# A decoder layer in FP32 on one core: the first two output-projection units begun together, the last two and the second norm in token halves

## What is computed

```python
merged = sigmoid(g_attn) * y_attn + sigmoid(g_pool) * y_pool     # (512, 1024)
x = x + gate1 * (merged @ w_out)                                  # w_out (1024, 1024)
h2 = rms_norm(x, norm2_g) * (1 + scale2) + shift2                 # mean of squares over the 1024 channels
up = h2 @ w_up                                                    # w_up (1024, 2 x 2816)
x = x + gate2 * ((silu(conv(up)_a) * conv(up)_b) @ w_down)
```

## Time and profile before

| | |
|---|---|
| median of 3 runs | 799.43 us (798.09 to 799.55) |
| span of the profiled execution, first to last instruction | 797.5 us |
| mean granted TensorE clock over the span | 0.989 |
| TensorE matmul busy | 97% |
| DVE, ACT, POOL busy | 47%, 38%, 44% |
| share of TensorE in the chain that ended last | 89% |

### The profile page before, as it was taken

The page is one execution under the profiler, slowest core; times in us unless marked ns, Lnnn a source line. Parts: engine busy times, 40 slices in busy tenths (PEclk is TensorE's granted clock), DMA queues, the critical chain, the costliest instruction groups (busy, mean ns, idle before and its releaser), DMA issues.

```text
span 797.5 us, 9523 instructions
## 1 busy us (share of the span) xinstructions
PE 772.9 (97%) x3618; PEld 622.3 (78%) x3618; DVE 371.7 (47%) x678; ACT 307.0 (38%) x492; POOL 353.5 (44%) x187
## 2 busy tenths in 40 slices
PE   4999999999999999998999999999999999999998
PEld 3367688887887888886886888888888888888886
DVE  2562399953656572448747444455443443000000
ACT  4234423346654553333233634434344344112121
POOL 1135258346534572354661544444344444444350
PEclk9979999999999999998999999999999999999999
DMA  8933112231043133454747333323333222232301
GB/s 322 356 106 107 53 53 67 94 106 44 10 159 106 53 110 102 151 165 159 227 143 263 106 106 106 95 74 95 106 106 95 78 93 93 92 106 93 120 27 53
DMA packets 94461, 91.72 MB, mean 115 GB/s; under 512 B 2003, under 2 KB 85711, under 8 KB 94415
## 3 DMA queue, kind: packets, MB, share of 16 engines
q1 hardware_dynamic: 92239, 82.71, 33.0%
q10 hardware_dynamic: 2176, 8.39, 3.1%
HBM read 89.00 MB, written 2.10 MB: 114 GB/s over the span
## 4 chain that ended last, share of the span: by engine, by line
PE 89%; DVE 7%; ACT 1%; issue 1%; DMA 1%; SPq 0%; ACTq 0%; DVEq 0%
PE bank L1368 49%; PE bank L1377 24%; PE bank L1589 3%; PE bank L1625 2%; DVE work L1153 2%; PE bank L1399 2%; DVE top L1150 2%; PE bank L1438 2%; PE bank L1600 2%; PE bank L1458 1%; PE bank L1404 1%; PE bank L1500 1%; DMA xn<-in_x_dram 1%; PE bank L1510 1%; DVE pmean L1187 1%
## 5 line engine op out<-in xcount | busy, mean ns | idle before, releaser
L583 POOL TENSOR_TENSOR wsplit<-stage,wsplit 128x1024 fp32r<-128x1024 f32 (+2 forms) x127 | 288.4, 2275 | 389.6 <-ACT wsplit L694 389.5
L1368 PE MATMUL bank<-hT,wsplit 128*128 128x512 f32 x1200 | 287.6, 391 | 0.0
L1368 PEld LDWEIGHTS bank<-hT,wsplit 128*128 128x128 f32 x1200 | 223.7, 188 | 46.6 <-issue 0.6
L694 ACT ACTIVATE wsplit<-stage 128x1024 fp32r<-128x1024 f32 (+2 forms) x127 | 125.6, 991 | 316.6 <-PE bank L1377 301.9
L1377 PE MATMUL bank<-hT,wsplit 128*128 128x512 f32 x600 | 150.8, 392 | 0.0
L1377 PEld LDWEIGHTS bank<-hT,wsplit 128*128 128x128 f32 x600 | 111.3, 188 | 24.2 <-issue 1.6
L1368 PE MATMUL bank<-guT,wsplit 128*128 128x512 f32 x352 | 84.0, 390 | 0.0
L1368 PEld LDWEIGHTS bank<-guT,wsplit 128*128 128x128 f32 x352 | 65.9, 188 | 13.5
L1330 DVE SCALAR_TENSOR_TENSOR yb<-bank,conv,yb 128x511 f32<-128x511 f32 (+1 forms) x44 | 33.0, 749 | 66.0 <-ACT yb L964 65.1
L1330 DVE SCALAR_TENSOR_TENSOR ya<-bank,conv,ya 128x511 f32<-128x511 f32 (+1 forms) x44 | 33.0, 750 | 60.1 <-ACT ya L964 59.4
L1355 DVE SCALAR_TENSOR_TENSOR xT<-bank,mod,xT 128x512 f32<-128x512 f32 x8 | 6.0, 751 | 111.5 <-PE bank L1377 111.5
(11 more groups left out here) (182 smaller groups left out, 837.4 us busy)
## 6 DMA issues: line engine op xcount, KB each, us to landing
stage<-in_w_up_dram SPq DMA_DIRECT2D x44, 512.0 KB, 5.2
stage<-in_w_in_dram SPq DMA_DIRECT2D x17, 1024.0 KB, 5.3
ada_mid<-in_w_ada_dram ACTq DMA_DIRECT2D x8, 1024.0 KB, 5.4
stage<-in_w_down_dram SPq DMA_DIRECT2D x8, 1024.0 KB, 5.1
ada<-in_w_ada_dram SPq DMA_DIRECT2D x7, 1024.0 KB, 12.3
stage<-in_w_ada_dram SPq DMA_DIRECT2D x4, 1024.0 KB, 5.6
stage<-in_w_out_dram SPq DMA_DIRECT2D x4, 1024.0 KB, 7.4
ada_last<-in_w_ada_dram SPq DMA_DIRECT2D x4, 1024.0 KB, 8.5
```

What stands on the lines that cost most here:

```text
L583: pool.tensor_tensor(unit_split(n, 1), unit_source(n), unit_split(n, 0).bitcast(F32), ALU.subtract).then_inc(low, 1)
L694: me.did(act.activation(unit_split(n, 0), unit_source(n), ACT.Copy), high)
L1368: pe.matmul(out_bank[:, :], hi[:, k, :], rhs[:, part, k0 + k, :], start=first and k == 0 and part == 0, stop=False)
```

## The change

**Head.** ("wo", 0) and ("wo", 1) are begun together, in three steps: blocks 0 to 5 of both, block 6 of both, block 7 of both. `mod_columns(3)` follows both. Orders on the other engines stay.

**Tail.** Units 6 and 7 are done for tokens 0 to 255 first (24 matmuls of 256 columns each), then `mod_columns(4)`, the squares of that half, then unit 6 for tokens 256 to 511 (into `PT[1]`), the roots of half 0, unit 7 for tokens 256 to 511 (into `PT[0]`). Residuals, squares, roots, norm and first up products are all done by halves; the up units 0 take half 0 with their low products two blocks behind, then half 1 with them one block behind. The squares of units 6 and 7 are summed by TensorE alone, so GpSimd adds five blocks instead of six. The units' `used` signal, which frees the ring, comes with their second half. `keep_clock` is gone.

**Both norms.** The square root takes scale 1/D and a bias tile `eps`, set by GpSimd at the start; the multiply-add ahead of it is gone.

```diff
@@ constants @@
+            pool.memset(eps[:, :], EPS).then_inc(consts, 1)
@@ gpsimd @@
-            for m in range(1, KD - 1):
+            for m in range(1, KD - 2):
                 low_parts(min(sch.unit["wo", m] + 3, sch.unit["wo", KD - 1] + 1))
@@ scalar @@
-            act.wait_ge(mean_ok, 1)
-            me.did(act.activation(tstat[:, 2, :], tstat[:, 1, :], ACT.Sqrt), root_ok)
+            def roots_of(n, tiles):
+                act.wait_ge(mean_ok, n)
+                me.did(act.activation(tstat[:, 2, tiles[0]:tiles[-1] + 1], tstat[:, 0, tiles[0]:tiles[-1] + 1],
+                                      ACT.Sqrt, bias=eps[:, 0:1], scale=1.0 / D), root_ok)
...
+            square_half(KD - 2, 0)
+            square_half(KD - 1, 0)
+            roots_of(2, HALF_TILES[0])
+            chunk(("wo", KD - 2))
+            square_half(KD - 2, 1)
+            for k in range(KD):
+                if k == 4:
+                    chunk(("wo", KD - 1))
+                    square_half(KD - 1, 1)
+                if k == KD - 1:
+                    roots_of(3, HALF_TILES[1])
+                h_high(KD + k, k, 3, HALVES[0])
+            for k in range(KD):
+                h_high(2 * KD + k, k, 3, HALVES[1])
@@ vector @@
+            for m in (KD - 2, KD - 1):
+                dve.wait_ge(wo_half, m - (KD - 2) + 1)
+                residual(m, 2, bank(("wo", m)), HALVES[0], x2_half)
             mod_vector(4)
+            half_roots(0)
+            await_chunk(dve, ("wo", KD - 2))
+            residual(KD - 2, 2, PT[1], HALVES[1], drained["dve"])
+            dve.wait_ge(root_b, 2)
             me.settle()
+            for k in range(KD):
+                norm_part(KD + k, k, 1, SC[0], HALVES[0])
+                if k:
+                    low_part(KD + k - 1, k - 1, 3, HALVES[0])
+                if k == 3:
+                    await_chunk(dve, ("wo", KD - 1))
+                    residual(KD - 1, 2, PT[0], HALVES[1], drained["dve"])
+            half_roots(1)
+            low_part(2 * KD - 1, KD - 1, 3, HALVES[0])
+            dve.wait_ge(root_b, 3)
...
@@ tensor @@
+            names = (("wo", 0), ("wo", 1))
+            for name in names:
+                await_bank(pe, name)
+            for ks in (range(KD - 2), range(KD - 2, KD - 1), range(KD - 1, KD)):
                 pe.wait_ge(m_lo, ks.stop)
-                high_products(sch.unit[first], bank(first), merged, ks=ks)
-                low_products(sch.unit[first], bank(first), merged, ks=ks)
-            for m in range(1, KD - 1):
+                for name in names:
+                    high_products(sch.unit[name], bank(name), merged, ks=ks)
+                    low_products(sch.unit[name], bank(name), merged, ks=ks)
+            mod_columns(3)
+            for m in range(2, KD - 2):
                 product(("wo", m), merged)
-                if m == 1:
-                    mod_columns(3)
+            ends = (("wo", KD - 2), ("wo", KD - 1))
+            for name in ends:
+                await_bank(pe, name)
+                high_products(sch.unit[name], bank(name), merged, tokens=HALVES[0])
+                low_products(sch.unit[name], bank(name), merged, tokens=HALVES[0], signal=wo_half)
             mod_columns(4)
...
-            keep_clock(6, qT[:, 0, 0, 0:P], qT[:, 0, 1, :])
...
+            name = ends[0]
+            high_products(sch.unit[name], PT[1], merged, tokens=HALVES[1])
+            low_products(sch.unit[name], PT[1], merged, tokens=HALVES[1])
+            spread_roots(NT + NT // 2, HALF_TILES[0], SC[0])
+            name = ends[1]
+            pe.wait_ge(mod_ok, 5)
+            high_products(sch.unit[name], PT[0], merged, tokens=HALVES[1])
+            low_products(sch.unit[name], PT[0], merged, tokens=HALVES[1])
...
+            for k in range(KD + 2):
+                if k < KD:
+                    first_high(names, k, KD + k, HALVES[0])
+                if k >= 2:
+                    first_low(names, k - 2, HALVES[0], None)
+                if k == 4:
+                    for part, m in ((1, KD - 2), (2, KD - 1)):
+                        pe.wait_ge(x2_sq, m + 3)
+                        mm = token_squares(part, sq2[:, m % 2, :], HALF_TILES[1])
+                    mm.then_inc(x2_sum, 1)
+                if k == KD - 2:
+                    spread_roots(2 * NT, HALF_TILES[1], SC[1])
+            for k in range(KD + 1):
+                if k < KD:
+                    first_high(names, k, 2 * KD + k, HALVES[1])
+                if k >= 1:
+                    first_low(names, k - 1, HALVES[1], used)
```

More of the change, by code:

```diff
@@ L64 @@
 ROW_LOADS = 11
+HALVES = (slice(0, S // 2), slice(S // 2, S))
+HALF_TILES = (range(NT // 2), range(NT // 2, NT))
 def index_steps(n):
@@ L229, in build_layer @@
         halves = place("halves", [P, 2], F32)
+        eps = place("eps", [P, 1], F32)
         vec = place("vec", [P, V_END], F32)
@@ L940, in _ @@
                     gate(m + 5)
-            for m in range(KD):
+            for m in range(KD - 2):
                 chunk(("wo", m))
@@ L1062, in mod_vector, with diagonals @@
                                                     in1=gain, op0=ALU.add, op1=ALU.mult))
[L1064 to L1068, removed]
+            def diagonals(n, tiles):
+                dve.wait_ge(root_ok, n)
+                part = slice(tiles[0], tiles[-1] + 1)
+                me.did(dve.reciprocal(tstat[:, 3, part], tstat[:, 2, part]))
@@ L1069, in roots @@
                 me.settle()
[L1070 to L1092, removed]
+                for t in tiles:
+                    me.did(dve.tensor_scalar(diag[:, t, :], ident[:, :], tstat[:, 3, t:t + 1], None, ALU.mult),
+                           diag_ok)
@@ L1100, in _ @@
             dve.wait_ge(x_sum, NT)
-            roots(0)
+            me.did(dve.tensor_copy(tstat[:, 1, :], tstat[:, 0, :]), mean_ok)
+            diagonals(1, range(NT))
             vectors()
@@ L1107, in _ @@
             dve.wait_ge(x_kept[0], KD // 2)
-            norm(0, 0)
+            dve.wait_ge(root_b, 1)
+            me.settle()
+            for k in range(KD):
+                norm_part(k, k, 0, SC[0], slice(0, S))
+                if k:
+                    low_part(k - 1, k - 1, 0, slice(0, S))
+            low_part(KD - 1, KD - 1, 0, slice(0, S))
             def low_of(out_ap, full, hi, signal):
@@ L1385, in product, with first_high, first_low @@
                 low_products(sch.unit[name], bank(name), rhs)
-            def first_products(names, which, lag):
-                for name in names:
[L1392 to L1409, removed]
+            def first_high(names, k, n, tokens):
+                for part, made in enumerate((h_hi, h_lo)):
+                    pe.wait_ge(made, n + 1)
+                    for name in names:
+                        if k == 0 and part == 0:
+                            pe.wait_ge(high, sch.unit[name] + 1)
+                        pe.matmul(bank(name)[:, tokens], unit_split(sch.unit[name], 0)[:, k, :],
+                                  hT[:, part, k, tokens], start=k == 0 and part == 0, stop=False)
+            def first_low(names, k, tokens, signal):
+                for name in names:
+                    pe.wait_ge(low, sch.unit[name] + 1)
+                    mm = pe.matmul(bank(name)[:, tokens], unit_split(sch.unit[name], 1)[:, k, :],
+                                   hT[:, 0, k, tokens], start=False, stop=k == KD - 1)
+                    if k == KD - 1 and signal is not None:
+                        mm.then_inc(signal, 1)
+            pe.wait_ge(consts, 12)
             pe.wait_ge(c_in, 16)
```

156 lines of the change are left out of this document (91 added, 65 removed).

## The result

Before: 799.01 us (median of 4 executions, 798.09 to 799.55). After: **819.6 us** (818.83 to 820.11). The ratio is 1.0267, 95% interval 1.0248 to 1.0285: 20.6 us slower by the medians, 21.3 by the ratio, where 2.6 were forecast and 805.5 was the upper end of the range.

A forecast was written before the change was run, and what follows sets the result against it. The prediction took TensorE, busy 97% of the span, to bound the kernel. Its terms, -1.3 and +3.0 in the head and +0.9 in the tail, summed to +2.6 us: 802.0 us forecast, range 797.5 to 805.5.

The forecast's parts named there:

- What bounds the kernel: Whole kernel: TensorE busy 97% of the span, so edits pay only where matmuls are not dense at full clock.
- Six dense products' worth: Tail: dense work of two output units and two up units, counted as 4 x 5.44 = 21.8 us.
- Edits at nothing: eps memset (0.1 us), first norm's square root without multiply-add, dropped clock-keeping matmuls and sixth addition of squares: no cost.
- Term 1: Head, output projection: beginning two units together saves 6.2 us of matmuls, but the columns start only 1.3 us earlier: -1.3.
- wait of 4.9: Head: TensorE idles from 376.2 to 381.1, 4.9 us, until vector 3's row lets the columns start.
- Term 2: Head, after the wait for the columns: half clock from 381.1 to about 386.5, costing +3.0 us.
- bound of 3.4: Head: the most that half clock after the wait would cost, 3.4 us, if all 6.8 us of it fell on work.
- Rival (a): Head: the clock stays full through the wait for the columns, 799.0 us, not slower; chance 0.08.
- Term 3: Tail, unit 5's end to the second up unit: 34.5 us against 33.6, +0.9, splits delaying low parts.
- rival (b): Tail: splits do not hold up the low parts, tail 31.8 us, total 799.3; chance 0.20.
- Rival (d): Tail: the half-filled norm stage loses the clock a second time, another 3 us, 805; chance 0.20.
- Sum: Head and tail together: -1.3 + 3.0 + 0.9 = +2.6 us.

The follow-up runs named there:

- head alone: Kernel before with only the change's head (units 0 and 1 begun together, vector 3's columns behind them), old tail and addresses: 800.74 us, ratio 1.0031.
- `eps` behind the arena: Kernel after with the eps tile moved to unused bytes behind the other tensors, which keep their old addresses: 804.15 us, ratio 1.0071.
- mended tail: Kernel after, old head and addresses; unit 6's second-half high products between vector 4's columns and squares, 8 unread matmuls ahead of blocks 0 and 4: 798.07 us, 1.0010.
- mended head: Kernel before with only the change's head, but the columns of vector 3 behind unit 2 instead of ahead of it: 794.7 us, ratio 0.9970.

## Why the prediction was wrong, point by point

- **What bounds the kernel: right, and not carried through.** TensorE is busy 97% of the time and dense products are nearly all of it. That says that a change of pace by 3% costs more than all that could be won in the head and tail. I priced the edits stretch by stretch and took 0.227 us as a constant of the program. ("Six dense products' worth" in the tail should read four; the sum there uses four.)
- **"Edits at nothing: the `eps` memset": the step that failed.** I costed the tile's instruction (0.1 us) and not its place. It was the largest term: 17 us (a pad of its size in the kernel before, 1.0215), against my nothing. The kernel and the full diff had what was needed to ask: `place` is sequential, and `eps` stands ahead of `hT`. That it would cost this much no row of before could show; the range could have been given room for it.
- **Term 1 (-1.3) and the wait of 4.9: right.** TensorE is idle for 4.6 us (4.7 in the head alone), and from the end of the branch products to the start of the columns are 15.8 us instead of 17.1. It is also shown by undoing: with the columns behind unit 2 the head is 4.9 us faster.
- **Term 2 (+3.0): right in kind, a little small.** Half clock lasted 10.3 us in the kernel after, 8.5 of it after the restart, where I took 5.4; columns and unit 2 took 1.7 and 2.4 us longer, 4.1 (4.3 in the trace of the head alone, 3.1 in that with `eps` behind the arena, where half clock lasted 6.8). The bound of 3.4 was passed in two of the three. In the head alone both terms gave +2.5 (1.4 to 3.5) against +1.7.
- **Rival (a)**, the clock staying full: did not occur in any of the five traces with the new head and its wait (half for 6.8 us in one, for about 10.2 in four). Behind the shorter stall of the old head it did, in three of twelve.
- **Term 3, the tail at 34.5: right where the clock holds**, 34.2 in the kernel after (at its slower pace) and 34.4 with the mended tail. A half matmul took 1.87 to 1.98 us for 16 in the kernel after, 0.117 to 0.124, and 1.91, 0.119, at the old distance; I took 0.12. The blocks of the second half come every 0.91 us, as taken. Both splits hold up a low part for 2 us, so rival (b) is out. Here the rule of the Trainium skill (SBUF — State Buffer, section Who interferes with whom), an exclusive lock for the whole instruction, is borne out: operations of 0.48 us took 2.01 and 1.98, while those that read PSUM stayed at 0.48.
- **Rival (d)**, a second loss of the clock: absent in the kernel after itself, present in the other six traces with this tail; at the old pace the tail then takes 38.0 and 38.1 us, +3.6, near my 3. I had placed its cause, the waits, between 16 and 23 of the tail. Of the two stretches of half clock only the second, from 24 to 31, lies behind those waits; the first, from 10 to 14, lies behind single-column matmuls.
- **Sum.** In the trace of the kernel after itself, head and tail together cost 3.9 us, 2.9 without the slower pace of six units, against the 2.6 of my sum; of the other 16.7 of the 19.6 us of span, 10.1 lie behind the second up unit, 1.0 in the six units and 5.7 ahead of the head (where this trace also has 3.6 us more at half clock, in the first 100 us). The runs apart agree: 17 (distance) + 2.5 (head) + 1 (tail with the clock full) give 20.5, against 20.6 measured.

## What to carry to other kernels

When a diff places a tensor, treat every address behind it as edited: compare the pace of a dense stretch that the diff does not touch, first of all, before explaining anything near the edit. In such a kernel a new small tile belongs behind the large ones, or the distance between the two operands of the hot matmuls is fixed by hand. When a stall is removed, look for the next item in the same queue and ask when its input is ready: here it was ready exactly when it had been needed, so a gain of 6.2 became 1.3 and cost the clock.

## What the runs showed of the hardware

- The start-to-start pace of 128x128 by 128x512 FP32 matmuls at full clock depends on the distance in SBUF between weights and moving operand: 0.227 us at the old distance and at 256 bytes more, 0.229 at 64, 0.232 to 0.233 at 32, 96, 128 and 192. Moving both together by 32 or 128 bytes changes nothing in the pace. The dense 512-column products from the up projection to the end follow it (10.1 us over 1,536 matmuls).
- With 256 columns the order of the distances is another: 0.119 to 0.120 us at the old one, 0.117 at 32 bytes more, 0.113 at 64, 0.119 to 0.120 at 128.
- The granted clock fell to half while TensorE was busy without a break, behind 3.5 us of matmuls with one column each (418.0 to 421.4 above), and behind 1.9 us of them in the mended head. In the kernel after the same 3.5 us were followed by full clock, so these runs do not show that such matmuls are the cause.
- Behind the same stall of 3.1 to 3.4 us of the old head, the clock was at half for 6.8, 3.4 or 0 us, by the execution.
